# Scores of the HGRN2 recurrence by chunk of 64 instead of by pairs of chunks

## The reference, cut to what matters

```python
a = jnp.einsum('bhnck,bhnsk->bhncs', q_c * jnp.exp(b_c - b_mid), k_c * jnp.exp(b_mid - b_c))
a = jnp.where(jnp.tril(jnp.ones((CHUNK, CHUNK), dtype=bool)), a, 0.0)
o_intra = jnp.einsum('bhncs,bhnsv->bhncv', a, v_c)
```

## Time and profile before

| what | value |
|---|---|
| median of three runs | 2157.39 us |
| the profiled execution | 2153.69 us, span 2151.9 us |
| PE busy | 2059.3 us (96%) |
| PEld busy | 1490.5 us (69%) |
| DVE busy | 1304.1 us (61%) |
| ACT busy | 931.9 us (43%) |
| POOL busy | 476.2 us (22%) |
| TensorE clock granted, mean | 0.989 |

### The profile page before, as it was taken

One profiled execution on the slowest core, in us unless ns is written; L12 is line 12 of the kernel. 1 busy time (PEld: TensorE's weight loads), 2 busy tenths in 40 slices (PEclk: granted clock), 3 DMA queues, 4 the chain that ended last, 5 costly groups with the idle time before them and its releaser, 6 DMA issues.

```text
span 2151.9 us, 30236 instructions
## 1 busy us (share of the span) xinstructions
PE 2059.3 (96%) x11372; PEld 1490.5 (69%) x11554; DVE 1304.1 (61%) x2360; ACT 931.9 (43%) x1960; POOL 476.2 (22%) x450
## 2 busy tenths in 40 slices
PE   5799999999999999999999999899999999999998
PEld 2567767767767767767767767677766666666665
DVE  7848648648648548548548548755563637465444
ACT  5746346346346346346356356344423131314222
POOL 2032222222222221221221222200161312100000
PEclk8899999999999999999999999999999999999999
DMA  7220110110110110110110110543321111204443
GB/s 278 79 69 11 45 55 11 45 54 11 45 54 11 46 53 11 47 53 11 54 45 11 60 40 1 186 147 122 123 71 50 45 51 33 88 10 148 147 147 117
DMA packets 106753, 144.45 MB, mean 67 GB/s; under 512 B 7136, under 2 KB 74224, under 8 KB 105584
## 3 DMA queue, kind: packets, MB, share of 16 engines
q1 hardware_dynamic: 99648, 125.72, 18.1%
q10 hardware_dynamic: 6960, 16.80, 2.0%
HBM read 108.91 MB, written 33.57 MB: 66 GB/s over the span
## 4 chain that ended last, share of the span: by engine, by line
PE 80%; ACT 7%; DVE 7%; issue 3%; DMA 2%; POOL 0%; SPq 0%; DVEq 0%; ACTq 0%; POOLq 0%
PE bank L1308 22%; PE bank L1309 21%; PE bank L1313 20%; PE bank L1464 4%; PE bank L1443 3%; PE bank L1475 3%; PE bank L1548 3%; PE bank L1450 2%; DVE xb L1074 2%; ACT xa L727 1%; ACT xa L729 1%; PE bank L1427 1%; ACT xb L737 1%; DVE xa L1038 1%; DMA ada_sb<-in_ada_w 1%
## 5 line engine op out<-in xcount | busy, mean ns | idle before, releaser
L1308 PE MATMUL bank<-h_hi,w_hi 128*128 128x512 f32 (+1 forms) x1472 | 576.6, 396 | 0.0
L1309 PE MATMUL bank<-h_hi,w_lo 128*128 128x512 f32 (+1 forms) x1472 | 550.6, 379 | 0.0
L1308 PEld LDWEIGHTS bank<-h_hi,w_hi 128*128 128x128 f32 x1472 | 279.3, 190 | 54.7
L1309 PEld LDWEIGHTS bank<-h_hi,w_lo 128*128 128x128 f32 x1472 | 279.3, 190 | 47.6
L1313 PE MATMUL bank<-h_lo,w_bf 128*128 128x512 bf16 (+1 forms) x1351 | 303.3, 365 | 7.9 <-issue 1.3
L1313 PEld LDWEIGHTS bank<-h_lo,w_bf 128*128 128x128 bf16 x1472 | 133.7, 98 | 142.7 <-issue 25.1
L1117 DVE SCALAR_TENSOR_TENSOR w_st<-w_st,cv,bank 128x128 f32<-128x128 f32 x560 | 194.2, 347 | 24.1 <-DVE w_st L1117 0.5
L1308 PE MATMUL bank<-wo_hi,og_hi 128*128 128x512 f32 x496 | 197.9, 399 | 3.1 <-DVE og_lo L1154 2.2
L1309 PE MATMUL bank<-wo_hi,og_lo 128*128 128x512 f32 x496 | 193.6, 390 | 0.0
L612 POOL TENSOR_TENSOR q<-qp,cv 128x512 f32<-128x512 f32 x64 | 71.9, 1124 | 524.9 <-PE bank L1443 244.1
L586 POOL TENSOR_TENSOR w_hi<-w_raw,zero_col 128x512 fp32r<-128x512 f32 x80 | 91.9, 1149 | 430.7 <-DMA w_raw<-in_w_in 228.7
(11 more groups left out here) (180 smaller groups left out, 3543.8 us busy)
## 6 DMA issues: line engine op xcount, KB each, us to landing
w_raw<-in_w_in SPq DMA_DIRECT2D x80, 256.0 KB, 2.8
ada_sb<-in_ada_w SPq DMA_DIRECT2D x8, 1024.0 KB, 13.9
xt<-in_x SPq DMA_DIRECT2D x16, 512.0 KB, 6.5
ada_a<-in_ada_late SPq DMA_DIRECT2D x64, 128.0 KB, 2.1
ada_b<-in_ada_late SPq DMA_DIRECT2D x64, 128.0 KB, 2.1
gated_scratch<-o_t ACTq DMA_DIRECT2D x32, 256.0 KB, 2.4
xr<-in_x SPq DMA_DIRECT2D x16, 512.0 KB, 5.0
x_scratch<-xr ACTq DMA_DIRECT2D x16, 512.0 KB, 2.6
```

Of the source, the lines that this page charges most:

```text
L1308: pe.matmul(out_ap, hi, m_hi, start=start, stop=False)
L1309: pe.matmul(out_ap, lo, m_hi, start=False, stop=False)
```

## The change

The scores are computed chunk by chunk. A chunk's scores are a product with 64 columns of `kp` as weights and 64 columns of `qp` moving, and lie in partitions 0 to 63 (even chunks) or 64 to 127 (odd chunks) of bank AB, in 4x64 columns instead of 4x128. Mask, masked copy, `am`, `am_b` and `asum` have 64 columns where they had 128. The value product takes 64 partitions of `asum` and `v_tok` to 64 partitions of the output, eight products instead of four. `w_st` and `am` change places in SBUF. The initial copy of the mask is two copies, one for each half of the partitions.

```diff
-        mask = place("mask", [P, 2, P], U8)
+        mask = place("mask", [P, 2, CHUNK], U8)
-        asum = place("asum", [P, 4, P], FP32)
+        asum = place("asum", [P, 4, CHUNK], FP32)
-        am = place("am", [P, 4, 4, P], FP32)
         w_st = place("w_st", [P, 16, P], FP32)
+        am = place("am", [P, 4, 4, CHUNK], FP32)
-        am_b = place("am_b", [P, 4, P], FP32)
+        am_b = place("am_b", [P, 4, CHUNK], FP32)
...
-            step(dve.tensor_copy(mask[:, :, :], maskf[:, :, :]))
+            for half in range(2):
+                rows = slice(half * CHUNK, (half + 1) * CHUNK)
+                step(dve.tensor_copy(mask[rows, :, :], maskf[rows, :, rows]))
...
                         dve.copy_predicated(am[:, ai, :, :] if d == 0 else am_b[:, :, :],
-                                            mask[:, d:d + 1, :].to_broadcast([P, 4, P]),
-                                            bank[AB][:, :].rearrange("p (a b) -> p a b", b=P)
+                                            mask[:, d:d + 1, :].to_broadcast([P, 4, CHUNK]),
+                                            bank[AB][:, 0:4 * CHUNK].rearrange("p (a b) -> p a b", b=CHUNK)
...
                             need(pe, "a_summed", 4, h, ai - 3)
-                            for j in range(4):
-                                last = pe.matmul(o[:, j * P:(j + 1) * P], asum[:, j, :], v_tok[:, 2 + 4 * b + j, :],
-                                                 start=False, stop=True, skip_group_check=True)
+                            for c in range(8):
+                                r = slice(c % 2 * CHUNK, (c % 2 + 1) * CHUNK)
+                                last = pe.matmul(o[r, c // 2 * P:(c // 2 + 1) * P], asum[r, c // 2, :],
+                                                 v_tok[r, 2 + 4 * b + c // 2, :], start=False, stop=True,
+                                                 skip_group_check=True)
...
                             need(pe, "a_masked", NA, h, ai)
-                            for j in range(4):
-                                last = pe.matmul(bank[AB][:, j * P:(j + 1) * P], kp[:, fi % 3, j * P:(j + 1) * P],
-                                                 qp[:, ai % 2, j * P:(j + 1) * P], start=(j == 0), stop=True,
+                            for c in range(8):
+                                r = slice(c % 2 * CHUNK, (c % 2 + 1) * CHUNK)
+                                t = slice(c * CHUNK, (c + 1) * CHUNK)
+                                last = pe.matmul(bank[AB][r, c // 2 * CHUNK:(c // 2 + 1) * CHUNK], kp[:, fi % 3, t],
+                                                 qp[:, ai % 2, t], start=(c < 2), stop=True,
                                                  skip_group_check=True)
```

## The result

The changed kernel takes 2132.0 us (median of four runs, 2130.78 to 2133.39) against 2156.13 us before (also four, 2153.93 to 2157.52): ratio 0.9892, 95% interval 0.9879 to 0.9904, that is 24 us less. Forecast were 2131 us and 24.3 us less.

A forecast was written before the change was run, and what follows sets the result against it. PE, busy 96% of the span, was taken to bound the kernel. Scores 20.4, values 1.8 and a DVE wait 2.1 sum to 24.3 us saved: 2153.7 + 1.8 - 24.3 = 2131 us, range 2123 to 2149.

The forecast's parts named there:

- The scores: L1475, score products: each counted group 0.37 us shorter (0.33 where transposes follow), 20.4 us in eight heads.
- The pair: Two 64-column score products side by side in the two halves of the array, L1475: 0.057 us.
- rival A: Pairs of small products run no closer than 0.108 us, so score groups cost 0.04 more; some 2154 us, chance 0.13.
- the change of shape: Switch of matmul shape that newly stands behind the score group, before the next product: 0.15 us.
- The first group of a head doesn't count: First of eight score groups, right before L1464's wait for the chain on DVE: its saving is nothing.
- The values: L1450, value products: 0.055 us saved a group, 32 times, 1.8 us.
- DVE: Masked copy 0.46 us, sum about 0.417; nearly all hidden behind PE, counting in one place, 2.1 us in all.
- the last wait: L1443 waiting for the chain behind the sum: chain starts 0.26 us sooner, 2.1 us in eight heads, bounds 0 and 4.
- The cover: Narrowest place, L1443 at 1005.51: PE gets 1.1 us ahead against a lead of 1.27 us, so DVE keeps up.
- The sum: Whole kernel: 20.4 + 1.8 + 2.1 = 24.3 us saved.
- The level: Executions seem to fall at either of two levels; median after put halfway: 2153.7 + 1.8 - 24.3 = 2131 us.
- The signs: Expected trace marks, such as score group 0.65 us instead of 0.77, score steps 8.7 instead of 9.05, L1128 near 0.46.

The follow-up runs named there:

- the experiment with DVE alone: The kernel before with only DVE's masked copy and sum cut to 64 of each 128 columns, products as before: 2155.08 us against 2155.62, ratio 0.9997.

## Why the prediction was right

- *The scores.* Forecast 0.37 us a group; measured 0.367 to the first matmul record of the narrow product (1.211 us from the first score record before, 0.844 after). The pair takes 0.058 (0.057 forecast), which puts rival A out, and the change of shape 0.15 (0.15). In the group of step 13 the next product is not the narrow but the wide one, with an fp32 load of 0.11: there it is 0.28 by the time the narrow one starts. In the last group of a head it is 0.38 to the transposes of the output (0.995 to 0.616), of which 0.05 is lost again behind them, which leaves the 0.33 forecast. 0.28 + 5x0.37 + 0.33 = 2.46 us a head, in all 19.7 us of the 20.4.
- *The first group of a head doesn't count.* From the first to the second score group it is 8.96 us before and 8.96 after; the following gaps are shorter by 0.28, 0.37, 0.37, 0.37, 0.45 and 0.45, the last two with 0.067 of the values in them.
- *The values.* 0.067 in 24 groups, near the 0.055. In the other 8, the last value group of a head, the transposes of the output follow (L1388), which have the full shape, as the old value product had: there the change adds a change of shape, and with what follows costs 0.08. I wrote that L1450 changes shape before and after in both kernels, which is wrong for these. 1.0 us instead of 1.8.
- *DVE.* The copy 0.44 (0.46 forecast), the sum 0.41 in the place that counts (0.42). But the last wait lost 0.10 us and not 0.26, because L1464 had ended only 0.16 us before the chain started (1045.65 against 1045.81), and the chain can't start before it: 0.8 us instead of 2.1. It was the one term for which I followed one predecessor of the chain and not the other; the earlier trace rows had no row of L1464 at that place.
- *The cover.* It held; the experiment with DVE alone shows the reverse side, that DVE's saving, but for those 0.8 us, is worth nothing by itself.
- *The sum.* 19.7 + 1.0 + 0.8 = 21.5 us, and the traces have 8x2.70 = 21.6. That is 2.8 less than the forecast, in three terms that were all too large (0.7, 0.8 and 1.3). The medians differ by 24, with an interval of 21 to 26 us. So the mechanism was right and its main term too, to 4%, while the two small terms were twice and nearly three times too large; that the 24.3 hit the medians so closely is in part luck. Where the 2 us beyond 21.6 lie, if they aren't chance, isn't shown; the wait early in a head and the lower clock behind it, which come in some executions oftener than in others, are a candidate.
- *The level.* I took the runs of before for two levels. With 22 runs of before they lie anywhere from 2152.97 to 2158.68, around 2155.6. The halfway point was right and its reason wrong. Of the 22, the nine up to 2155.21 us with a mean granted clock of 0.989 to 0.991 are all shorter than the eleven with 0.984 to 0.987 (2155.72 and more), so the spread goes with how much of an execution ran at the lower clock. (In a later set of nine that is less clear: two with 0.990 took 2156.28 and 2157.33.)
- *The signs.* I wrote that the score group takes 0.65 us from first to last start instead of 0.77. The 0.65 was counted from the last record of L1464, and the first 0.20 don't belong to it: it is 0.46 instead of 0.885, as the terms had it. Of the others x1024, x512 with two records 0.007 us apart, steps of 8.68 us and L1128 at 0.44 came as written. L1097 takes 0.63 in the mean and not up to 0.6, the wait before L1464 in the first such group of a head grew from 0.87 to 1.15, by 0.28 and not 0.37 (the product behind that group is the wide one), and the last wait moved by 0.10.

The Trainium skill, "TensorEngine Tiling (Array Packing)", Key Properties, has the change of mode drain TensorE: here 0.15 to 0.20 us from the last record to the next load, and one of them less in a step was worth 0.14. Its Gotcha 1 (row tiles must not use one bank at the same time) didn't show as a stall where the two wrote different partitions of the bank.

## What to carry to other kernels

Price small fp32 matmuls by four numbers out of the trace: streaming by columns, load by weight columns, whether neighbours use different parts of the array, and the changes of shape between groups; here they gave the main term of the gain to 4%. Put groups of one shape next to each other and alternate the halves within a group. For each wait, follow all of its predecessors before a saving on one of them is counted. And look at what else stands in the steps in which PE does wait (here two of the sixteen partial sums, beside POOL, and the transfers that queue behind them): moving it gave half as much again as the change itself.

## What the runs showed that I had not expected

- Products in one half of the array start ahead of products of the other half that stand before them in the program. With the even chunks first and the odd ones after, a second series of score records, 0.058 us apart like the first, begins 0.287 us after it, 6 ns behind its fifth record of eight; the first series' last three start at 0.340, 0.398 and 0.456 us. The last record so starts at 0.75 us, where 0.46 is the paired order and about 0.93 would be one half after the other. The value group does the same (the second series at 0.493 us, its fifth predecessor at 0.487). That a series is a half I infer from the spacing; the records don't name it. The Trainium skill, "TensorE: Matmul & The Clock Gate", Step-by-step: what each phase is for, says that matmuls stay in program order and only weight loads are pulled ahead; the trace doesn't agree with it for products in different halves. Why the second series waits for five records of the first is open.
- DVE's partial sums of 0.48 us take 0.82 to 1.33 us (once 1.51) where POOL splits weights beside them, and the clamp of 256 elements, 0.29 us in the first head with no splitting beside it, 1.12.
- A wait of some 2 us can cost more than itself: in the head of before that lasts 161.1 us the wait is 0.7 us longer than in its neighbours (2.22 against 1.54), and the lower clock behind it takes another 0.6.
